# A hybrid attention, RG-LRU and expert step on one core: fused minima in attention, pair sums on VectorE, gate weights in two buffers, first slabs in parts, 32 expert dots in the placing stage

## What is computed

```python
def layer(x, mod):                       # once for context tokens, once for latent ones
    h = rmsnorm(x) * (1 + scale) + shift
    q, k, v, xr, yr = split(h @ w_in)    # 5 x 512 features
    att = attention(q, k, v)             # 8 heads of 64; context: softmax over 256 keys
    # latent: a window of 8 rows of the 64-wide grid with a relative bias, and the 256 cached keys
    xc = depthwise_conv(xr)
    r, i = sigmoid(xc @ w_a), sigmoid(xc @ w_i)      # in both directions, 64x64 blocks
    h = scan(a = exp(8 * r * log_sigmoid(lam)), b = sqrt(1 - a*a) * i * xc)
    x = x + gate * (concat(att, (h_f + h_b) * gelu(yr)) @ w_out)
    h = modulate(rmsnorm(x))
    s = (h @ w_q) . sub_keys             # 8 heads, two halves, 128 keys each
    best = top16 of the pair sums of top16 and top16 -> 128 experts of 16384 a token, with shares
    return x + gate * sum_e share_e * gelu(h . u[e]) * v[e]
```

## Time and profile before

| | us |
|---|---|
| median of 3 runs | 4169.16 |
| lowest and highest | 4165.14, 4172.41 |
| the profiled execution's own time | 4164.17 |
| its span, first to last instruction | 4162.4 |
| TensorE busy, mean granted clock | 3298.2 (79%), 0.897 |
| VectorE, ScalarE, GpSimd busy | 2691.0, 1041.5, 1993.6 |
| context: projection, attention | 172.2, 31.2 |
| context: output projection, routing | 56.8, 115.5 |
| latent: projection, attention | 353.7, 321.0 |
| latent: output projection, routing | 172.0, about 558 |
| placing, with the store behind it | about 252 |
| experts, final norm | about 2016, 59 |

### The profile page before, as it was taken

How to read it: one execution, slowest core, us unless ns; L and a number is a source line. 1 busy time by engine, 2 the same in 40 slices (tenths; PEclk the granted TensorE clock), 3 DMA queues, 4 the chain that set the end, 5 groups by cost and what they waited for, 6 DMA issues and landing times. The chain is left out here.

```text
span 4162.4 us, 47342 instructions
## 1 busy us (share of the span) xinstructions
PE 3298.2 (79%) x15160; PEld 2205.1 (53%) x15160; DVE 2691.0 (65%) x5751; ACT 1041.5 (25%) x1780; POOL 1993.6 (48%) x1987
## 2 busy tenths in 40 slices
PE   5776888788896878757536678989899989999993
PEld 3545334567642323336525456666666666666662
DVE  2136676777554665678667777777777767776445
ACT  4431133344211000036511122222222222222111
POOL 0002554322234777630044466676776766676450
PEclk8888899899897999868768789999999999999997
DMA  7422766644566787735587799999999999999996
GB/s 256 149 76 83 240 212 225 180 140 143 187 213 227 279 287 275 271 127 159 148 300 276 269 355 383 375 362 372 384 386 377 395 366 378 375 382 356 361 346 252
DMA packets 404104, 1136.99 MB, mean 273 GB/s; under 512 B 33792, under 2 KB 121088, under 8 KB 403712
## 3 DMA queue, kind: packets, MB, share of 16 engines
q0 software_dynamic: 221184, 805.40, 53.2%
q1 hardware_dynamic: 182784, 329.91, 22.3%
HBM read 1079.60 MB, written 55.58 MB: 273 GB/s over the span
## 5 line engine op out<-in xcount | busy, mean ns | idle before, releaser
L2117 POOL DMA_INDIRECT exp_key_row<-in_u_rows,exp_u_id x512 | 617.7, 1206 | 393.2 <-DVE exp_dot L2171 211.9
L2171 DVE CUSTOM_DVE_ANT_0 exp_key_row<-exp_key_row,exp_x 128x1024 f32<-128x1024 f32 x512 | 621.9, 1220 | 189.5 <-DMA exp_key_row<-in_u_rows,exp_u_id 152.6
L2125 POOL DMA_INDIRECT exp_value_row<-in_v_rows,exp_v_id x512 | 573.2, 1120 | 327.0 <-issue 157.0
L354 POOL DMA_INDIRECT ahead_row<-in_u_rows,keep_expert_id x256 | 323.7, 1265 | 500.2 <-DVE keep_dot L364 435.9
L2036 PE MATMUL exp_o_ps<-exp_v_hi,exp_w_hi 128*128 128x512 f32 x1024 | 347.1, 422 | 226.5 <-DVE exp_acc L2234 209.4
L2021 PE MATMUL exp_a_ps<-exp_xT_hi,exp_u_hi 128*128 128x512 f32 x1024 | 411.0, 401 | 62.5 <-DVE exp_xT_lo L2149 50.2
L2234 DVE TENSOR_TENSOR exp_acc<-exp_o_ps,exp_acc 128x1024 f32<-128x1024 f32 x256 | 311.4, 1221 | 149.2 <-PE exp_o_ps L2036 125.0
L2021 PE MATMUL exp_a_ps<-exp_xT_lo,exp_u_hi 128*128 128x512 f32 x1024 | 403.7, 394 | 0.0
L2021 PE MATMUL exp_a_ps<-exp_xT_hi,exp_u_lo 128*128 128x512 f32 x1024 | 401.7, 392 | 0.0
L2036 PEld LDWEIGHTS exp_o_ps<-exp_v_hi,exp_w_hi 128*128 128x128 f32 x1024 | 198.1, 201 | 330.0 <-DVE exp_acc L2234 259.4
L364 DVE CUSTOM_DVE_ANT_0 ahead_row<-ahead_row,ahead_x 128x1024 f32<-128x1024 f32 x256 | 306.7, 1221 | 78.2 <-DMA ahead_row<-in_u_rows,keep_expert_id 74.8
(11 more groups left out here) (374 smaller groups left out, 5471.7 us busy)
## 6 DMA issues: line engine op xcount, KB each, us to landing
exp_u_raw<-in_uT SPq DMA_DIRECT2D x130, 512.0 KB
exp_v_raw<-in_v_rows SPq DMA_DIRECT2D x128, 512.0 KB
scratch_g<-place_grid SPq DMA_DIRECT2D x4, 8192.0 KB, 30.5
exp_g_raw<-scratch_g SPq DMA_DIRECT2D x128, 256.0 KB
proj_ctx_mod_slab<-in_w_mod SPq DMA_DIRECT2D x8, 2048.0 KB
proj_ctx_slab<-in_w_in SPq DMA_DIRECT2D x10, 1024.0 KB, 5.2
proj_lat_slab<-in_w_in SPq DMA_DIRECT2D x10, 1024.0 KB, 9.7
mod_slab<-in_w_mod SPq DMA_DIRECT2D x4, 2048.0 KB, 20.2
```

The costliest lines, as they stand in the source:

```text
L354: nc.gpsimd.indirect_dma_start(out=ahead.row[:, n % KEY_RING, :], out_offset=None, in_=io["u_rows"], in_offset=bass.IndirectOffsetOnAxis(a ...
L2117: nc.gpsimd.indirect_dma_start(out=key_row[:, j % RING, :], out_offset=None, in_=io["u_rows"], in_offset=bass.IndirectOffsetOnAxis(ap=u_id ...
L2125: nc.gpsimd.indirect_dma_start(out=value_row[:, 4 * (j % 2) + t, :], out_offset=None, in_=io["v_rows"].rearrange("a b n -> (a b) n"), in_o ...
L2171: nc.vector.tensor_tensor_reduce(out=key_row[:, j % RING, :], in0=key_row[:, j % RING, :], in1=x[:, :], scale=1.0, scalar=0.0, op0=ALU.mul ...
```

## The change

- Projection: gate weights in two buffers with a semaphore each. Loads 0 and 1 stand at the start, load `a + 1` where load `a` stood. `r` moves into the memory of `routes[1]`. The copy of the queries is scaled by 1/8.
- Attention: heads go in pairs. Scores of a head contract over its own 64 rows (no `q_own`), the products of the two halves are issued alternately into two PSUM buffers. VectorE makes the cached part first, `min(-(s + 0))` with the write of the negated scores, then the local part, `min(-(s + bias))` starting from the first minimum, each in one `tensor_tensor_reduce`; copy and maximum are gone. The exponential is in place with scale -1, scores in a ring of three, transposed probabilities in a ring of four. Values are the stationary operand now: the product is the transposed output, two heads in the two column halves. The shares are spread by a matmul with the identity (`share_columns`), asked for ahead of the scores of the next pair and copied by ScalarE, and VectorE multiplies into `catT` (`place`). No barrier between tiles. Cached keys are loaded ahead of the bias and counted on `k_in`, values on `v_in`, waited for at the second pair. The dots are dealt out by pairs.
- Output projection: `w_out` in two halves with a semaphore each.
- Routing: the first slab in four parts of 128 columns; the keys are waited for behind the first queries. VectorE makes the pair sums of both units, GpSimd only the key steps; the hits are collected at the end of the turn.
- Placing: GpSimd gathers 32 expert rows of the first gathered latent tile, VectorE takes one dot a step; the first eight expert rounds hold 12 dots instead of 16.

```diff
@@ projection_and_rg_lru
-        weights = s.sb("weights", [P, 4, P])
+        weights = s.sb("weights", [P, 2, 4, P])
...
             load_weights(0)
+            load_weights(1)
...
-                if a >= 1:
+                if 1 <= a < RG_TILES - 1:
                     sp.wait_ge(product, PRODUCTS * a)
-                    load_weights(a)
+                    load_weights(a + 1)
@@ attention
+                for at, w, keys in pieces:
+                    for half in range(2):
+                        rows = slice(64 * half, 64 * half + 64)
+                        mm = nc.tensor.matmul(s_ps[half][:, at:at + w], fused[rows, Q0 + j, b * P:(b + 1) * P],
+                                              keys[rows, :], start=True, stop=True)
...
+                for c, (at, w) in enumerate(chunks):
+                    for half in range(2):
...
+                        last = nc.tensor.matmul(o_ps[64 * half:64 * half + 64, 0:P], values,
+                                                probT[0:w, (2 * i + half) % TURNED, c, :],
+                                                start=(c == 0), stop=(c == len(chunks) - 1))
...
+            scores(0)
+            for i in range(len(STEPS)):
+                turn(i, 0)
+                if i:
+                    share_columns(i - 1)
+                if i + 1 < len(STEPS):
+                    scores(i + 1)
+                turn(i, 1)
+                if i == 1 and not context:
+                    pe.wait_ge(v_in, 16)
+                if i:
+                    weigh(i - 1)
...
+            for i in range(len(STEPS)):
+                exp(i, 0)
+                exp(i, 1)
+                move(i, 0)
+                if i:
+                    copy_share(i - 1)
+                move(i, 1)
...
+                for half in range(2):
+                    head = 2 * j + half
+                    dve.wait_ge(own, marks[half])
+                    nc.vector.tensor_tensor_reduce(
+                        out=out[half][:, 0:width], in0=s_ps[half][:, 0:width],
+                        in1=bias[:, head, :, :].rearrange("p j c -> p (j c)")[:, offset * GRID_W:offset * GRID_W + width],
+                        scale=-1.0, scalar=low_ctx[:, n % 2, head:head + 1], op0=ALU.add, op1=ALU.min,
+                        accum_out=low[:, n % 2, head:head + 1]).then_inc(low_ready, 1)
...
+            lowest(0)
+            for i in range(len(STEPS)):
+                if i + 1 < len(STEPS):
+                    lowest(i + 1)
+                shares(i)
+                dots(i)
+                if i:
+                    place(i - 1)
@@ out_projection
+            for half in range(2):
+                cut = slice(half * SLAB, (half + 1) * SLAB)
+                sp.dma_start(w[:, :, cut], io["w_out"].rearrange("(j p) n -> p j n", p=P)[:, :, cut]).then_inc(w_in[half], 16)
@@ routing
-            sp.dma_start(slab[:, 0, :, :], w_q[:, :, 0:SLAB]).then_inc(slab_in[0], 16)
+            for ct in range(4):
+                cut = slice(ct * P, (ct + 1) * P)
+                sp.dma_start(slab[:, 0, :, cut], w_q[:, :, cut]).then_inc(first_in[ct], 16)
...
-                for x in range(2):
-                    prepare(c, unit + x, x)
-                    values(1)
+                steps(c, unit)
+                values(2)
...
+                c.wait()
+                dve.sem_inc(tops_ready, 1)
+                pair_sums(c)
+                c.wait()
+                marks = [c.n, c.n]
                 for x in range(2):
-                    dve.wait_ge(cand_ready, unit + x + 1)
                     phase(x, largest(0, cand, 2, best))
...
+                if unit:
+                    for x in range(2):
+                        c.step(collect(unit - 2 + x, x))
@@ place_weights
+                for n in KEYS[PLACE_DOTS * before // TOTAL:PLACE_DOTS * (before + 1) // TOTAL]:
+                    key_dot(nc, ahead, dve, n)
@@ experts
+    FIRST, TURN = 8, SLOTS // BATCH
+    WIDE = (SLOTS - PLACE_DOTS) // FIRST
...
                 if wide:
-                    DOT(); DOT(); DOT()
+                    DOT(); DOT()
```

461 lines of the change are left out of this document (234 added, 227 removed).

## The result

| | before | changed |
|---|---|---|
| median, us | 4167.15 (4 runs, 4151.29 to 4172.41) | 3875.40 (4 runs, 3867.32 to 3885.31) |
| ratio | | 0.9307, 95% interval 0.9272 to 0.9342 |
| span of the profiled execution, us | 4162.4 | 3869.7 |
| mean granted clock of TensorE | 0.897 | 0.914 |

The kernel is 7% faster, 28 us beyond the 3903 us that were forecast and inside the range. To see where it went I cut both spans at the first matmul of each stage, as the order of time gives it; the last stretch runs to the span's end. What TensorE waits for at a seam therefore counts to the stage ahead of it. The forecast's terms are put in the same stretches: the seam ahead of the latent attention was to shrink by 12.5 us (22.5 to 10), so -33 - 12.5 stand at the latent projection and -82.5 at the attention.

What follows compares the result with a forecast made beforehand. No single engine was taken to bound the whole kernel; gains come from waits in the first 2426 us, before a DMA-bound stretch. Terms sum to -268 us from 4164.2, 3896, with 5.0 to the median 3901, stated as 3903; range 3855 to 3985.

Steps and rivals of the forecast that it cites:

- +18: Placing: one added dot in each of 32 steps hides only in part, +0.55 us a step, +18 us in all.
- Gate weights: Both projections: a second weight buffer removes TensorE's stalls whole, latent -33 us, context -9 us.
- Attention: Latent attention: a pair of heads on both array halves takes 6.7 us, -95 us; context attention -4 us.
- First slabs in parts: Work starts on the first part loaded: output projection -7 us latent, -4 context; routing -6 latent, -4 context.
- Join: Latent routing: pair sums on VectorE cut a turn from 31.5 to 27 us, -67 us; context routing +3 us.
- Dots: First eight expert rounds: four dots fewer each, from 39 to about 31.5 us a round, -60 us.
- the floor: First eight expert rounds: the least a round can take is 29.3 us, as in the 48 rounds behind them.
- A: Attention: array halves run one after another, 9.7 us a pair, total 3988 us; chance 0.10.
- B: Attention: packing is imperfect, scores and weighing 30% dearer, total 3928 us; chance 0.05.
- C: Latent routing stays at 31 us a turn, gathers and products on hits holding each other, total 3970 us; chance 0.12.
- D: Moving dots gains nothing: placing pays 38 us, rounds give back only 4.6 us of work; total 3946 us; chance 0.14.
- E: Attention: changes of tile form empty the array for long; at 2 us each, total 4270 us, slower; chance 0.04.

Runs made afterwards that it cites:

- the version with all four: Changed kernel with share columns behind the scores, 64 dots in placing, one latent product on hits on VectorE, output weights split by rows: 3821.8 us, ratio 0.9164.

## Why the prediction was right, and where its terms were off

The total is nearer than its parts. By stretch the forecast is off by 46 us on the side of too little gain and by 21 on the other, and 25 of 293 is what is left; the +18 that never came stands against 14 us too many at the latent output projection and routing. That part is luck.

**Gate weights.** Right: no stall, latent projection -35 alone (33 said). In the context group I counted the wait, 9, and forgot the clock that I had counted in the latent one. It measured 15 alone, 6 of them products that ran faster.

**Attention.** The mechanism was right: both halves run at once. I said 6.7 us a pair; it is about 5.5 us in tiles of eight rows and 6.06 in those of nine. A nine-row pair is 0.91 + 0.37 for the first transposes and the share columns, 1.72 for the scores (1.57 said), 0.91 for the other transposes and 2.15 for the weighing (1.8 said); these are distances between starts, so the five changes of form are in them. TensorE has no wait in it, and of the 6.7 us the 0.4 for the loop were not needed, and 0.24 of the 6.3 for TensorE. In eight-row tiles, which I did not price apart, its work is 5.0 us and it still waits 0.4 to 0.65 a pair for an exponential. The fused operations cost 7 and 60 ns more than the plain ones, nearer my bound of 0 than that of 0.3 us. Part of the gain was given back at the front, where I counted 12 us for the first wait and the end: from the scores of one pair to those of the next the first four take 15.8, 11.6, 8.6 and 8.9 us, until the bias has come and 2.3 us of mask are added, and TensorE's first transposes wait 11.4, 5.6, 2.7 and 2.3 us for exponentials. In the context attention I said 27 us for eight pairs at 3.3; it is 32. A pair takes 4.07 us at first and 2.77 later; in the order of time of TensorE the same four records of scores stand with both durations:

```profile
218.22 1.23 PE L967 MATMUL att_ctx_s_ps<-cheads_fused 64*128 64x256 f32 x4
...
229.66 0.70 PE L967 MATMUL att_ctx_s_ps<-cheads_fused 64*128 64x256 f32 x4
```

The granted clock is 0.50 from 212 to 222 us and 1.00 from 228 to 240: TensorE, which had idled 8.3 us at the seam, works at the lower level, 1.2 GHz, for the first pairs and at 2.4 GHz behind them.

**First slabs in parts.** Context -11.4 (8 said), right in kind. The latent output projection gave 1 us instead of 7: the step that failed was that a half lands in half the time and the other meanwhile. Beside gathers, with rows shorter than theirs, it landed after 12.1 us and the other after 25.8. In the latent routing the wait fell from 8.6 to 2.0 us as said, but without the parts the stage is only 1 to 3.5 us longer; that values arrive later than the queries are made, and take the rest, was not tested.

**Join.** 27.5 us a turn where I said 27, from the queue of GpSimd: with one product moved off it the turn fell to 26.0 us. In the version with all four the same move gave nothing, so this rests on one program. VectorE now waits for the hits, as named. Context +4.0 (3 said).

**Dots.** The rounds came out as said, from 39.2 to 31.3 us, -63 us for 8 against -60; another 7 us of the stretch lie in the 48 untouched rounds, 29.4 and 29.3 us each. The reason was right too: 4.9 us of VectorE's work and 4.0 us of its waits for gathered rows leave a round, and 0.8 come back as waits for TensorE (16.1 and 22.3 us over the eight). Only the floor was wrong, by 6 us. The placing's +18 was the largest error, and the step that failed is the overlap. I read 1 us of slack a step, charged the dot with its duration, 1.2 us, and let only half of it hide. The waits with a releaser come to 22.6 us and 9.5 at L1744, 1.0 us a step. The operations of a step take 5.53 us from start to start when nothing waits (2.77 for each two batches), and a step took 6.71 on average, between 5.5 and 7.8; so 1.2 us were free, and a dot, from its start to the next one's, holds VectorE 1.14. It fitted: nearly all steps now take 6.67 us.

**Rivals.** A is not what happens. By its own figures it should have stood at 3903 + 32 x 3.0 = 3999 us, not 3988. B: the scores took 1.7 us for both heads and the weighing 2.15, 0.5 us a pair more than said, with the changes of form in them, and the pair still came out shorter. (30% of 3.37 us is 1.0 and not 0.8 us, and 32 x 1.0 is 33 and not 25.) It is not overlap that is missing: the records of the two halves start 6 to 7 ns apart. The figure of 3.07 for four row tiles in the Trainium skill, "TensorE: Matmul & The Clock Gate", section "Measured speedup vs the span model", is for another number of tiles; for two halves this trace shows no loss of that size. C, a routing that stays at 31 us, did not happen, nor D. E: seven transposes with a change of form behind them take 0.92 us (852.76 to 853.68) where the earlier trace rows have 0.76 without, and a pair with one change fewer is 0.20 us shorter, so a change costs 0.16 to 0.2 us, as the earlier trace rows had it.

## What to carry to other kernels

The slack of an engine in a step is the step less the distances between the starts of its instructions, not the sum of its named waits; work that fits into it is free, and one more piece costs its full distance. Before a floor is taken from other rounds, compare what the engines do in them. Products on two halves of the array are best alternated in the queue: one half after the other cost 40 us here. And a load that is cut to arrive sooner has to keep its rows as long as those of the transfers that it competes with.

## What the runs showed of the hardware that was not expected

Products on disjoint halves of the array, alternated in the queue, started 6 to 7 ns apart: both heads' scores (halves of the rows) took 1.7 us and the weighing (halves of the columns) 2.15 us, against 2.7 and 3.35 with one half after the other. In that order too the second half starts early, beside the product two places ahead of it in the queue; two score products a half lose nothing (1.5 us in both orders), three lose 1 us.

VectorE's product on 1024 elements with two operands takes 1.21 us, but 2.67 us where it began during GpSimd's product on hits (1257.83, 2.37 us long): it ended within 0.1 us of when it would have if it had started at the end of the other. From the version with all four, in the order of time:

```profile
1257.83 2.37 POOL L1575 TENSOR_TENSOR route_lat_hit<-route_lat_hit,route_lat_key_step 128x1024 f32<-128x1024 f32 x1
...
1258.62 2.67 DVE L1627 TENSOR_TENSOR route_lat_hit<-route_lat_hit,route_lat_key_step 128x1024 f32<-128x1024 f32 x1
```

It is no matter of length: a sum of 64 elements of VectorE (L1636), 0.22 us elsewhere, took 1.99 us when it began 0.5 us into such a product, at 1232.46. Reductions with one operand that began during one in the changed kernel (1224.80) took 0.69 us, as elsewhere.

"GPSIMD Engine Reference" of the Trainium skill, section "Specifications", has GpSimd share its SBUF interfaces with VectorE, with contention for VectorE instructions with two SBUF inputs. The trace agrees, with 1.5 us more for this one.
